# A hybrid decoder step on one core: wide state steps, later selection rounds, another order at the opening of a head pair, another last norm

## The chip, the cores and the metric

The kernel runs on one core of one Trainium2 chip, in one launch. The metric is the device time of that core in microseconds (us). The engines named below are PE (TensorE: matmuls; each has a weight load before it), DVE (VectorE), ACT (ScalarE), POOL (GpSimd) and SP (SyncE, which here only issues DMAs).

## What is computed

One decoder layer for 256 prompt tokens and 8 requests of 4 new tokens each, 288 columns in all. Everything is float32.

```python
c_rw, c_att, c_gate = split(rmsnorm(x, norm1) @ w_in)
o_rw, wkv_new, shift_new = rwkv7_mix(c_rw, ...)      # 16 heads of 64: a recurrence over tokens
#   S = S*w_t + (S a_t) b_t^T + v_t k_t^T ;  y_t = S r_t
o_att = attend(rope(q), rope(k), v, ...)             # each query keeps its 64 best keys by an indexer's scores
merged = sigmoid(g_rw) * (o_rw @ p_rw) + sigmoid(g_att) * (o_att @ p_att)
h = x + merged @ w_o
h = h + (silu(conv(gate)) * up) @ w_down             # gate, up = split(rmsnorm(h, norm2) @ w_up)
y = rmsnorm(h, norm_f)                               # also out: keys, values, states, last rows
```

## The kernel before

**Blocks.** Every weight matrix is cut into units of 128 output columns, and a unit into 16 blocks of 128 x 128 (11 for `w_down`). Weights and activations are split into a high and a low part, and a block (`blocks`, L621 to L623) is three matmuls of 128 x 128 weights on 288 columns. Per unit n, SP loads the weights into one of two slots as soon as unit n-2's low part has been made, ACT copies out the high part (`split_hi`, L587), DVE subtracts to get the low part (`split_lo`, L567, or in four parts, L579), and PE waits for that (`w_split`) before the unit's first block.

**Blocks as filling.** The attention and the recurrence have small matmuls between which DVE and ACT must work. There PE does blocks of other units meanwhile, in numbers written by hand: `fill_cols(count)` with the `FILL_...` constants in the attention (24 units, 384 blocks), `fill(count)` in a head pair (4 units, 64 blocks). A higher number at one place means a lower one later, since what is left is done at the end. DVE keeps a count of the same blocks: `streamed(count)` adds to it and issues the `split_lo` of filling unit m+2 once the count is at least 16(m+1)+5. So the place of each split in DVE's order follows from these constants. All waits are in order on each engine.

**Selection.** `eight_best` marks eight best scores (a maximum and a replacement). The second query tile's scores, `ACC[:, 1]`, take eight such rounds and two more operations (`marks_to_bias`), in `select`, which stands ahead of the six attention steps (`ATT_STEPS`: sample 0, first tile twice, second tile twice, sample 1). Their `BIASP[:, 1]` is first read in step 3.

**A head pair.** 8 passes of a loop (7 and a last one), two heads each, 64 tokens per chunk. PE opens with eight transposes of b, k, v and the read vectors into tokens-by-channels form (banks 2 and 3), then the decayed products in small tiles, `fill(5)`, and the first of the products that invert a triangular matrix (`blockwise`, L945), for which DVE must have made a mask and its transpose (`block16`). At that point DVE is still finishing the pair before: in its order stand the low part of a unit, a reciprocal and four operations on `YS`, and only then the mask. Later in the pair three state steps carry the state from chunk to chunk: PE waits for `state`, does four matmuls of 64 x 64 x 64 for the next state and four for the outputs, then `fill(2)`.

**The end.** The last norm: the square sums go through an all-ones matmul of 288 columns to all partitions (`last_sum`), DVE adds epsilon, ACT takes the root, DVE the reciprocal of 128 x 288, and multiplies `YO` by it in five parts, each of which ACT then sends out.

Of the kernel before, what the change touches and what calls it, by code (L numbers as in the profile page):

```python
# [23 lines left out]
P = 128  # L24
# [172 lines left out]
Y_PARTS = (slice(0, 4), slice(4, 8), slice(8, 12), slice(12, 14), slice(14, 16))  # L197
# [66 lines left out]
def build(nc, a, o):  # L264
# [58 lines left out]
    QZ = m("q_grouped", [P, KVH, 4, AH, DS])  # L323
    sel_at = m.at
    ACC = m("scores", [P, 2, SEQ])
# [48 lines left out]
    MT = m("chunk_map", [P, 4, CH])  # L374
# [17 lines left out]
    LO = m("l_off", [P, 2, 2 * BL])  # L392
    MLS = region(vv_at)("m_low_s", [NS, 2, NS])
# [23 lines left out]
    HRSTD = m("h_rstd", [P, N])  # L417

# [5 lines left out]
    FRSTD = m("f_rstd", [P, N])  # L424
# [22 lines left out]
    with ExitStack() as ctx:  # L447
# [34 lines left out]
        def _(sp):  # L482
            sp.dma_start(NORMS[:], a["norms"]).then_inc(sem("norms_in"), 16)

# [10 lines left out]
            load_x(12, 16, "x_in3")  # L495
# [99 lines left out]
        def _(pe):  # L595
# [281 lines left out]
            def pair(it, last=False):  # L877
# [25 lines left out]
                for w, src in enumerate((BT, KTL, RKV[:, 2, :], AR[:, 0, :])):  # L903
                    for tt in range(2):
                        ins = tr(BK[2 + tt][:, w * P:(w + 1) * P], src[:, tt * P:(tt + 1) * P], ident)  # L905
                ins.then_inc(sem("tok_mm"), 1)
# [16 lines left out]
                ins.then_inc(sem("b_mm"), 1)  # L923
                pe.wait_ge(sem("bonus"), v)
# [12 lines left out]
                fill(5)  # L937
# [11 lines left out]
                pe.wait_ge(sem("tok_sb"), v)  # L949
                pe.wait_ge(sem("block16"), v)  # L950
                settle(pe)
                blockwise(2, L1, U)
                fill(3)
                pe.wait_ge(sem("inv_l"), v * 8 - 7)
                settle(pe)
                blockwise(3, L2, UT, True)
# [3 lines left out]
                blockwise(2, L1, UT, True)  # L960
                fill(3)
                pe.wait_ge(sem("inv_l"), v * 8 - 5)
                settle(pe)
                blockwise(3, L2, T)
# [11 lines left out]
                for tt in range(2):  # L976
                    for e in range(2):
                        for par, r in enumerate(halves):
                            c0 = (0, 2 * P)[e] + tt * CH
                            mm(BK[(4, 2)[e]][halves[par ^ e], c0:c0 + CH], MK[r, 2 * e + tt, 0:CH],  # L980
                               TOK[r, tt, 2, e * HD:(e + 1) * HD], start=True, stop=True)
# [11 lines left out]
                fill(3)  # L993
                for merge in range(2):
# [44 lines left out]
                    fill(3)  # L1039
# [18 lines left out]
                fill(2)  # L1058
# [27 lines left out]
                ins.then_inc(sem("state_s_mm"), 1)  # L1086
                for c in range(1, NCH):
                    tt, par = divmod(c, 2)
# [3 lines left out]
                    settle(pe)  # L1092
                    for e, h in enumerate(halves):
                        ins = grown(grow, 0, tt, MT[h, c, :], ST[h, c - 1, :], e, par)
                    ins.then_inc(sem("state_mm"), 1)
                    if c == 1:
                        pe.wait_ge(sem("read"), v)
                        settle(pe)
                    for e, h in enumerate(halves):
                        ins = grown(read, 0, tt, ST[h, c - 1, :], QT[h, c, :], e, par)  # L1100
                ins.then_inc(sem("y_mm"), 1)
                fill(2)
                if not last:
# [110 lines left out]
            last_sum(2, FSUM, FSQ)  # L1214
# [3 lines left out]
        def _(act):  # L1218
            act.dma_start(WRAW[:, 0, 0:4, :].rearrange("p k c -> p (k c)"),
# [3 lines left out]
            for dst, src in ((PRM_ALL, "pair_params"), (LMU, "lora_mu")):  # L1223
                act.dma_start(dst[:], a[src]).then_inc(sem("params_in"), 16)

# [40 lines left out]
            act.dma_start(AC[:], a["att_c"]).then_inc(sem("att_c_lora_in"), 16)  # L1266
            actv(ROOT[:, 0:1], MEANS[:, 0:1], ACT.Sqrt)
# [203 lines left out]
            def pair(it, last=False):  # L1471
# [15 lines left out]
                act.wait_ge(sem("tok_mm"), v)  # L1487
                actv(flat(TOK[:, 0]), BK[2][:], ACT.Copy)
                actv(flat(TOK[:, 1]), BK[3][:], ACT.Copy).then_inc(sem("tok_sb"), 1)
# [9 lines left out]
                def evac(k):  # L1499
                    act.wait_ge(sem("inv_mm"), v * 8 - 8 + k)  # L1500
                    actv(flat(L2[:]), BK[2][:, 0:4 * BL], ACT.Copy).then_inc(sem("inv_u"), 1)
                act.wait_ge(sem("m1_mm"), v)
                for rows, other in both_halves:
                    ins = actv(TOK[rows, :, 1, HD:P], BK[2][other, 2 * P:3 * P].rearrange("p (t f) -> p t f", t=2), ACT.Copy)
# [161 lines left out]
            norm_root(2, FRSTD)  # L1666
# [56 lines left out]
        def _(dve):  # L1723
# [207 lines left out]
            st.done(marks_to_bias(early, BIASP[:, 0, 0:P], causal[0]))  # L1931
            select(ACC[:, 1, :], TOPK_P, BIASP[:, 1, :], causal[1], FILL_TOPK).then_inc(sem("bias_ready"), 1)
            dve.wait_ge(sem("bias_ready"), 1)

# [565 lines left out]
```

## Time and profile before

| | us |
|---|---|
| median of 3 runs | 1784.6 (1784.6 to 1786.84) |
| the profiled execution's own time | 1784.55 |
| its span | 1783.0 |
| PE busy | 1762.4 |
| DVE busy | 1119.2 |
| ACT busy | 759.8 |

A line of the time line gives start, duration, engine, line of the kernel, operation, output<-inputs, shape and count. A matmul's duration is its modelled time through the array; the next one starts before it ends, so the pace of PE is read from the starts, not from the durations or from the busy share. A float32 matmul outside the blocks is recorded as two passes, so its count is twice that of the order of instructions; a transpose is one pass.

### The profile page before, as it was taken

The page shows a single profiled execution, that of the slowest core. Times are in us where ns is not written, and L with a number is a line of the kernel's source. Part 1 is how long each engine was busy: PE and PEld are TensorE (multiplying, and loading weights), DVE is VectorE, ACT ScalarE, POOL GpSimd, SP SyncE. Part 2 cuts the span into 40 slices and gives each one's busy share as a digit, 9 for nine tenths or more (in the row PEclk, how much of TensorE's full clock was granted, in tenths as well). Part 3 has the DMA queues.
Part 4 walks back from the last instruction along what each step waited for, and adds up shares of the span by engine and source line. Part 5 has one row for each costly group of instructions (what it writes and reads, how often), then busy time and mean ns, then how long its engine had stood idle before and what let it go on. Part 6 is the DMA issues. An engine that isn't in the chain of part 4 may idle for free.

```text
span 1783.0 us, 40707 instructions
## 1 busy us (share of the span) xinstructions
PE 1762.4 (99%) x16500; PEld 1704.9 (96%) x16500; DVE 1119.2 (63%) x1995; ACT 759.8 (43%) x1059; POOL 53.6 (3%) x103
## 2 busy tenths in 40 slices
PE   9999999999999999999999999999999999999997
PEld 8999899988888888999999999999999999999996
DVE  7764954667777777765566666666666665444444
ACT  6456444555555554433443333333333333333332
POOL 2500000000000000000000000000000000000000
PEclk9999999999999999999999999999999999999999
DMA  7644344433332333644454444444444444555553
GB/s 279 227 162 163 130 160 152 155 114 107 108 107 104 111 108 113 222 166 151 174 219 165 165 165 165 165 165 165 165 165 165 165 165 162 175 169 174 169 170 132
DMA packets 51696, 283.46 MB, mean 159 GB/s; under 512 B 7248, under 2 KB 11856, under 8 KB 25776
## 3 DMA queue, kind: packets, MB, share of 16 engines
q1 hardware_dynamic: 43632, 260.35, 41.7%
q10 hardware_dynamic: 3744, 12.56, 2.0%
q0 software_dynamic: 4256, 9.65, 1.8%
q8 instruction: 46, 0.75, 0.2%
q14 instruction: 18, 0.15, 0.0%
HBM read 274.26 MB, written 8.27 MB: 158 GB/s over the span
## 4 chain that ended last, share of the span: by engine, by line
PE 95%; DVE 3%; DMA 1%; ACT 0%; issue 0%; DVEq 0%; SPq 0%
PE bank L621 30%; PE bank L623 28%; PE bank L622 28%; PE bank L945 1%; PE bank L985 1%; DVE w_lo L567 1%; DVE scores L1919 1%; PE bank L852 0%; PE bank L905 0%; DVE max L1886 0%; DMA x_raw<-in_x 0%; PE bank L800 0%; PE bank L817 0%; PE bank L1046 0%; PE bank L642 0%
## 5 line engine op out<-in xcount | busy, mean ns | idle before, releaser
L621 PE MATMUL bank<-x_split,w_lo 128*128 128x288 f32 x2880 | 873.2, 303 | 3.3 <-DVE w_lo L567 2.1
L622 PE MATMUL bank<-x_split,w_hi 128*128 128x288 f32 x2880 | 849.5, 295 | 0.0
L623 PE MATMUL bank<-x_split,w_hi 128*128 128x288 f32 x2880 | 847.0, 294 | 0.0
L587 ACT ACTIVATE w_hi<-w_raw 128x2048 fp32r<-128x2048 f32 (+1 forms) x262 | 468.8, 1789 | 590.9 <-PE bank L623 578.7
L567 DVE TENSOR_TENSOR w_lo<-w_raw,w_hi 128x2048 fp32r<-128x2048 f32 (+1 forms) x238 | 503.8, 2117 | 283.7 <-ACT w_hi L587 283.4
L621 PEld LDWEIGHTS bank<-x_split,w_lo 128*128 128x128 f32 x2880 | 540.2, 188 | 20.3 <-issue 9.6
L622 PEld LDWEIGHTS bank<-x_split,w_hi 128*128 128x128 f32 x2880 | 541.0, 188 | 1.8 <-issue 0.7
L623 PEld LDWEIGHTS bank<-x_split,w_hi 128*128 128x128 f32 x2880 | 542.2, 188 | 0.0
L621 PE MATMUL bank<-act_split,w_lo 128*128 128x288 f32 x704 | 208.5, 296 | 0.0
L622 PE MATMUL bank<-act_split,w_hi 128*128 128x288 f32 x704 | 207.7, 295 | 0.0
L623 PE MATMUL bank<-act_split,w_hi 128*128 128x288 f32 x704 | 207.0, 294 | 0.0
L623 PEld LDWEIGHTS bank<-act_split,w_hi 128*128 128x128 f32 x704 | 132.6, 188 | 0.0
L622 PEld LDWEIGHTS bank<-act_split,w_hi 128*128 128x128 f32 x704 | 132.2, 188 | 0.0
L621 PEld LDWEIGHTS bank<-act_split,w_lo 128*128 128x128 f32 x704 | 131.9, 187 | 0.2 <-DVE w_lo L567 0.2
L621 PE MATMUL bank<-merged_split,w_lo 128*128 128x288 f32 x256 | 75.9, 297 | 0.0
L622 PE MATMUL bank<-merged_split,w_hi 128*128 128x288 f32 x256 | 75.5, 295 | 0.0
L623 PE MATMUL bank<-merged_split,w_hi 128*128 128x288 f32 x256 | 75.3, 294 | 0.0
L579 DVE TENSOR_TENSOR w_lo<-w_raw,w_hi 128x512 fp32r<-128x512 f32 x96 | 62.1, 682 | 1.2
L2356 DVE TENSOR_TENSOR conv<-bank,h_rstd 128x288 f32<-128x288 f32 x44 | 20.1, 457 | 67.8 <-PE bank L623 67.8
L1301 ACT ACTIVATE cols<-bank 128x256 f32<-128x256 f32 x40 | 15.4, 384 | 90.6 <-PE bank L623 90.6
L2339 DVE TENSOR_TENSOR gate_ext<-bank,h_rstd 128x256 f32<-128x256 f32 x44 | 18.7, 425 | 52.9 <-PE bank L623 52.9
L621 PEld LDWEIGHTS bank<-merged_split,w_lo 128*128 128x128 f32 x256 | 48.0, 187 | 0.4 <-issue 0.2
(390 smaller groups left out, 1537.9 us busy)
## 6 DMA issues: line engine op xcount, KB each, us to landing
w_raw<-in_w_up SPq DMA_DIRECT2D x88, 1024.0 KB, 4.8
w_raw<-in_w_in SPq DMA_DIRECT2D x47, 1024.0 KB, 4.9
w_raw<-in_w_down SPq DMA_DIRECT2D x64, 704.0 KB, 4.0
w_raw<-in_w_gate SPq DMA_DIRECT2D x32, 1024.0 KB, 4.9
w_raw<-in_w_p SPq DMA_DIRECT2D x16, 1024.0 KB, 4.8
w_raw<-in_w_o SPq DMA_DIRECT2D x16, 1024.0 KB, 4.8
h<-in_x ACTq DMA_DIRECT2D x1, 2304.0 KB, 10.3
h_spill<-h ACTq DMA_DIRECT2D x1, 2304.0 KB, 9.6
```

The costliest lines, as they stand in the source:

```text
L567: eng.tensor_tensor(WLO[:, slot, 0:kt], WRAW[:, slot, 0:kt], WHI[:, slot, 0:kt].bitcast(F32), ALU.subtract).then_inc(sem("w_split"), 1)
L579: ins = dve.tensor_tensor(WLO[:, slot, k], WRAW[:, slot, k], WHI[:, slot, k].bitcast(F32), ALU.subtract)
L587: actv(WHI[:, slot, 0:kt], WRAW[:, slot, 0:kt], ACT.Copy).then_inc(sem("w_hi"), 3 if isinstance(n, int) and n == 2 else 1)
L621: mm(out, wl, hi, start=first and k == ks[0], stop=False, skip_group_check=True)
L622: mm(out, w, lo, start=False, stop=False, skip_group_check=True)
L623: ins = mm(out, w, hi, start=False, stop=last and k == ks[-1], skip_group_check=True)
L945: ins = mm(BK[bank][q, u * w:(u + 1) * w], lhs[q, u], rhs[q, u], start=True, stop=True)
L985: return mm(BK[banks[par]][halves[e], c0:c0 + CH], lhs, rhs, start=start, stop=False, skip_group_check=True)
L1301: actv(tile[:, 1:1 + SEQ], BK[j % 2][:, 0:SEQ], ACT.Copy)
L1919: ins = V.scalar_tensor_tensor(acc, src, w, acc if i or par else causal[qt], ALU.mult, ALU.add)
L2339: V.tensor_tensor(gx[:, 2:2 + SEQ], BK[0][:, 0:SEQ], HRSTD[:, 0:SEQ], ALU.mult)
L2356: st.done(V.tensor_tensor(c[:, 0:N], BK[1][:, 0:N], HRSTD[:], ALU.mult))
```

## The change

The parts, in program order:

- Start: the norm gains are loaded by ACT's queue, no longer first by SP's; two parameter loads of ACT move later; SP issues the last quarter of `x` behind the load of unit 2, and the constants behind the load of unit 3.
- Attention: the constants of the filling change (selection of the samples 25 to 33 blocks, `FILL_TOPK` 30 to 12, `FILL_SAMPLE` 14 to 16, `FILL_SOFTMAX` 14 to 15). The eight rounds of the second tile are taken out of `select` and put into the attention steps: three after the probabilities of step 0, two after the maximum of step 1, three and the bias after the probabilities of step 1.
- Pair: the products stand first; of the transposes k and v follow them and b and a come later, behind the third inversion product; `fill(5)` goes, and the five blocks are given to `fill` calls further on and to the rest at the end (15 to 16 blocks).
- State steps: the map and the state are kept as 128 x 128 matrices with zeros off the two heads' blocks, and a step is one matmul of 128 x 128 weights on 64 columns. The outputs of a chunk come one step later.
- Last norm: the sums are taken to tokens-by-two form, root and reciprocal are of 128 x 6, and three diagonal matrices and three matmuls spread the result; `YO` is multiplied from the bank, in parts of 2, 3, 4, 4 and 3 tiles.

```diff
-Y_PARTS = (slice(0, 4), slice(4, 8), slice(8, 12), slice(12, 14), slice(14, 16))
+Y_PARTS = (slice(0, 2), slice(2, 5), slice(5, 9), slice(9, 13), slice(13, 16))
-FILL_ROPE, FILL_REQUESTS, FILL_TOPK_S, FILL_TOPK, FILL_SAMPLE = 12, 2, 25, 30, 14
+FILL_ROPE, FILL_REQUESTS, FILL_TOPK_S, FILL_TOPK, FILL_SAMPLE = 12, 2, 33, 12, 16
-FILL_SCORES, FILL_SOFTMAX, FILL_P_T, FILL_PV = 8, 14, 5, 4
+FILL_SCORES, FILL_SOFTMAX, FILL_P_T, FILL_PV = 8, 15, 5, 4
...
                 if isinstance(n, int) and n == 2:
+                    load_x(12, 16, "x_in3")
+                if isinstance(n, int) and n == 3:
                     sp.dma_start(MC[:], a["main_c"]).then_inc(sem("main_c_in"), 16)
...
                 for c in range(1, NCH):
                     fill(2)
+                    if c > 1:
+                        pe.wait_ge(sem("read"), v * 4 - 4 + c)
+                        both_heads(read, c - 1, STB[:, c % 2, :], QT[:, c - 1, :])
                     pe.wait_ge(sem("state"), v * 4 - 4 + c)
                     pe.wait_ge(sem("map"), v)
+                    both_heads(grow, c, MTB[:, c - 1, :], ST[:, c - 1, :]).then_inc(sem("state_mm"), 1)
...
+                    if which == 0:
+                        late_rounds(0, 3)
                     streamed(FILL_SCORES + FILL_SOFTMAX)
...
+                if n == 1:
+                    late_rounds(5, 8)
+                    st.done(marks_to_bias(late, BIASP[:, 1, :], causal[1]))
                 streamed(FILL_SCORES + FILL_SOFTMAX)
...
+            for tt in range(3):
+                V.tensor_scalar(FDIAG[:, tt, :], ident, FROOT[:, tt, 0:1], float(D_MODEL), ALU.mult, ALU.mult).then_inc(sem("norm_ms"), 1)
```

On PE at the opening of a pair in the loop, before (`b_t`, `k_t`, `rkv`, `ar` on the constants are the transposes, `ar,b_t` and the like the products, `u_and_t,l` the inversion):

```order
L1137 UNCONDITIONAL_BRANCH
L1137 ISA
L905 MATMUL bank<-main_consts,b_t 128x128 x2
L905 MATMUL bank<-main_consts,k_t 128x128 x2
L905 MATMUL bank<-main_consts,rkv 128x128 x2
L905 MATMUL bank<-main_consts,ar 128x128 x2
L912 MATMUL bank<-ar,b_t 32x32 x16
L916 MATMUL bank<-ar,b_t 64x64 x8
L921 MATMUL bank<-ar,k_t 64x128 x8
L929 MATMUL bank<-b_t,ar 64x32 x8
L933 MATMUL bank<-ar_s,bk_v_s 64x64 x2
L936 MATMUL bank<-main_consts,bk_v_s 128x128
```

Five blocks and then L945 follow. The same place now:

```order
L1145 UNCONDITIONAL_BRANCH
L1145 ISA
L919 MATMUL bank<-ar,b_t 32x32 x16
L923 MATMUL bank<-ar,b_t 64x64 x8
L928 MATMUL bank<-ar,k_t 64x128 x8
L912 MATMUL bank<-main_consts,k_t 128x128 x2
L912 MATMUL bank<-main_consts,rkv 128x128 x2
L937 MATMUL bank<-b_t,ar 64x32 x8
L941 MATMUL bank<-ar_s,bk_v_s 64x64 x2
L944 MATMUL bank<-main_consts,bk_v_s 128x128
L952 MATMUL bank<-u_and_t,l_108 32x32 x16
```

The first inversion product stands right behind the opening, and four of the eight transposes are gone from it.

On DVE in attention steps 0 and 1, before (the splits are `w_lo`):

```order
L1948 SCALAR_TENSOR_TENSOR prob<-softmax_stats,att_consts 128x16
L1951 TENSOR_SCALAR prob<-prob,softmax_stats 128x256
L567 TENSOR_TENSOR w_lo<-w_raw,w_hi 128x2048
L1958 SCALAR_TENSOR_TENSOR prob<-bank,bias_prompt 128x512
L1962 TENSOR_REDUCE softmax_stats<-prob 128x4
L567 TENSOR_TENSOR w_lo<-w_raw,w_hi 128x2048
L1965 RECIPROCAL softmax_stats<-softmax_stats 128x4
```

And now:

```order
L1980 TENSOR_SCALAR prob<-prob,softmax_stats 128x256
L1910 MAX max_79<-scores 128x8
L1913 MATCH_REPLACE scores<-max_79,scores 128x256
L1910 MAX max_79<-scores 128x8
L1913 MATCH_REPLACE scores<-max_79,scores 128x256
L1910 MAX max_79<-scores 128x8
L1913 MATCH_REPLACE scores<-max_79,scores 128x256
L571 TENSOR_TENSOR w_lo<-w_raw,w_hi 128x2048 x2
L1989 SCALAR_TENSOR_TENSOR prob<-bank,bias_prompt 128x512
L1993 TENSOR_REDUCE softmax_stats<-prob 128x4
```

Three rounds stand between the probabilities of step 0 and the splits, and two splits stand together.

## Rows read from the trace of the kernel before

**Rows 1.** The page: span, then busy time of each engine.
```profile
span 1783.0 us, 40707 instructions
PE 1762.4 (99%) x16500; PEld 1704.9 (96%) x16500; DVE 1119.2 (63%) x1995; ACT 759.8 (43%) x1059; POOL 53.6 (3%) x103
```
**Rows 2.** Time line of PE (start, us, operation, count), from one pair into the next.
```profile
482.18 0.65 PE L1111 MATMUL bank<-y,main_consts 128*128 128x288 f32 x2
...
494.77 0.38 PE L905 MATMUL bank<-main_consts,b_t 128*128 128x128 f32 x2
...
495.73 0.35 PE L912 MATMUL bank<-ar,b_t 64*32 64x32 f32 x32
...
497.27 0.38 PE L621 MATMUL bank<-x_split,w_lo 128*128 128x288 f32 x1
...
499.57 0.45 PE L945 MATMUL bank<-u_and_t,l 32*32 32x32 f32 x32
```
**Rows 3.** Time line of DVE in the same stretch.
```profile
482.94 0.46 DVE L2221 SCALAR_TENSOR_TENSOR y<-bank,y 128x288 f32<-128x288 f32 x1 [1.14 <-PE bank L1111]
...
487.23 1.95 DVE L2054 RECIPROCAL squares_k<-squares_k 128x288 f32<-128x288 f32 x1
...
494.58 1.95 DVE L2235 RECIPROCAL y_sq<-y_sq 128x288 f32<-128x288 f32 x1
...
499.15 0.31 DVE L2106 STREAM_TRANSPOSE l<-u_and_t 128x128 f32<-128x128 f32 x1
```
**Rows 4.** Time line of PE: a state step, and the end of the three.
```profile
521.24 0.33 PE L985 MATMUL bank<-state,chunk_map 64*64 64x64 f32 x4
521.62 0.40 PE L621 MATMUL bank<-x_split,w_lo 128*128 128x288 f32 x1
...
522.61 0.33 PE L985 MATMUL bank<-state,chunk_map 64*64 64x64 f32 x4
...
525.45 0.82 PE L852 MATMUL bank<-lora,cols 128*128 128x128 f32 x5
```
**Rows 5.** Time line of PE: six float32 passes with 128 x 128 weights, then a block.
```profile
485.23 0.61 PE L870 MATMUL bank<-main_consts,decay_tok 128*128 128x130 f32 x4
485.67 0.31 PE L871 MATMUL bank<-main_consts,decay_tok 128*128 128x40 f32 x2
485.81 0.38 PE L621 MATMUL bank<-x_split,w_lo 128*128 128x288 f32 x1
486.03 0.29 PE L622 MATMUL bank<-x_split,w_hi 128*128 128x288 f32 x1
```
**Rows 6.** Time line of DVE: two rounds' starts, and the probabilities of step 0.
```profile
221.82 0.43 DVE L1886 MAX8 max<-scores 128x8 f32<-128x256 f32 x1
...
222.80 0.43 DVE L1886 MAX8 max<-scores 128x8 f32<-128x256 f32 x1
...
239.88 0.35 DVE L1951 TENSOR_SCALAR prob<-prob,softmax_stats 128x256 f32<-128x256 f32 x1
```
**Rows 7.** Time line of ACT: the unit's end at 234.79, and the first exponential.
```profile
234.79 0.39 ACT L1301 ACTIVATE cols<-bank 128x256 f32<-128x256 f32 x1 [2.02 <-PE bank L623]
...
238.86 0.48 ACT L1377 ACTIVATE prob<-bank,softmax_stats 128x260 f32<-128x260 f32 x1
```
**Rows 8.** Time line of PE in the selection: its longest wait for a split.
```profile
218.90 0.40 PE L621 MATMUL bank<-x_split,w_lo 128*128 128x288 f32 x1 [0.89 <-DVE w_lo L567]
```
**Rows 9.** Time line of PE in the first 34 us: the wait for unit 2.
```profile
23.04 0.40 PE L642 MATMUL bank<-x_split,w_lo 128*128 128x288 f32 x1 [1.36 <-DVE w_lo L567]
```
**Rows 10.** Time line of PE and DVE in the last norm.
```profile
1770.17 0.75 PE L610 MATMUL bank<-f_squares,mean_ones 128*128 128x288 f32 x2 [0.53 <-ACT f_squares L1658]
...
1771.93 1.95 DVE L1737 RECIPROCAL f_rstd<-f_rstd 128x288 f32<-128x288 f32 x1 [0.51 <-ACT f_rstd L1274]
1773.91 5.23 DVE L2394 TENSOR_TENSOR y_out<-y_out,f_rstd 128x1152 f32<-128x1152 f32 x5
```
**Rows 11.** Stretches after the last matmul: us, PE busy (x), granted clock, DMA share, GB/s.
```profile
1771.00:1775.40 4.40, 0.00 (x0) 1.00 0.00 0
1775.40:1783.00 7.60, 0.00 (x0) 0.50 0.77 310
```

More of the change, by code:

```diff
@@ L902, in pair, with turned @@
                 pe.wait_ge(sem("ar_ready"), v)
[L903 to L906, printed above, removed]
+                settle(pe)
+                def turned(bank, sources):
+                    for w, src in enumerate(sources):
+                        for tt in range(2):
+                            ins = tr(BK[bank][:, (2 * tt + w) * P:(2 * tt + w + 1) * P], src[:, tt * P:(tt + 1) * P], ident)
+                    ins.then_inc(sem("tok_mm"), 1)
                 chunks = [(tt, par) for tt in range(2) for par in range(2)]
@@ L1086, in pair, with both_heads @@
                 ins.then_inc(sem("state_s_mm"), 1)
+                def both_heads(banks, c, lhs, rhs):
+                    tt, par = divmod(c, 2)
+                    return mm(BK[banks[par]][:, tt * CH:(tt + 1) * CH], lhs, rhs, start=False, stop=False, skip_group_check=True)
                 for c in range(1, NCH):
-                    tt, par = divmod(c, 2)
                     fill(2)
+                    if c > 1:
+                        pe.wait_ge(sem("read"), v * 4 - 4 + c)
+                        both_heads(read, c - 1, STB[:, c % 2, :], QT[:, c - 1, :])
                     pe.wait_ge(sem("state"), v * 4 - 4 + c)
                     pe.wait_ge(sem("map"), v)
[L1092 to L1101, printed above, removed]
+                    both_heads(grow, c, MTB[:, c - 1, :], ST[:, c - 1, :]).then_inc(sem("state_mm"), 1)
                 fill(2)
+                pe.wait_ge(sem("read"), v * 4)
+                both_heads(read, NCH - 1, STB[:, 0, :], QT[:, NCH - 1, :]).then_inc(sem("y_mm"), 1)
                 if not last:
@@ L1501, in evac @@
                     actv(flat(L2[:]), BK[2][:, 0:4 * BL], ACT.Copy).then_inc(sem("inv_u"), 1)
+                act.wait_ge(sem("tok_mm"), v * 2)
+                actv(TOK[:, :, 0:4:3, :], BK[6][:].rearrange("p (t w f) -> p t w f", t=2, w=2), ACT.Copy).then_inc(sem("tok_sb"), 1)
                 act.wait_ge(sem("m1_mm"), v)
                 for rows, other in both_halves:
[L1504 removed]
+                    ins = actv(TOK[rows, :, 1, HD:P], BK[3][other, 2 * P:3 * P].rearrange("p (t f) -> p t f", t=2), ACT.Copy)
                 ins.then_inc(sem("m1_odd"), 1)
@@ L1665, in _ @@
             down_units(KT // 2 - 1, 2 * DU - 2)
-            norm_root(2, FRSTD)
+            act.wait_ge(sem("norm_sq_used"), KT * 3)
+            actv(FROOT[:].rearrange("p t x -> p (t x)"), BK[2][:, 0:6], ACT.Sqrt, bias=EPSC[:]).then_inc(sem("norm_rms"), 1)
             for i, k in enumerate(Y_PARTS):
@@ L1930, in _, with late_rounds @@
                     eight_best(early, TOPK_P - 8 * heads[1])
-            st.done(marks_to_bias(early, BIASP[:, 0, 0:P], causal[0]))
-            select(ACC[:, 1, :], TOPK_P, BIASP[:, 1, :], causal[1], FILL_TOPK).then_inc(sem("bias_ready"), 1)
+            marks_to_bias(early, BIASP[:, 0, 0:P], causal[0]).then_inc(sem("bias_ready"), 1)
             dve.wait_ge(sem("bias_ready"), 1)
+            streamed(FILL_TOPK)
+            late = ACC[:, 1, :]
+            def late_rounds(r0, r1):
+                for r in range(r0, r1):
+                    eight_best(late, TOPK_P - 8 * r)
             for n, (kind, which) in enumerate(ATT_STEPS):
@@ L2147, in pair @@
                 inv(4)
-                add_t(blocks(3), 4)
+                add_t(blocks(2), 4)
                 V.transpose(L1[:], T).then_inc(sem("inv_l"), 1)
@@ L2183, in pair, with state_blocks @@
                 split_part(dve, n + 2, 0, 3)
+                def state_blocks(c):
+                    tt, par = divmod(c, 2)
+                    for e, h in enumerate(halves):
+                        ins = V.tensor_scalar(STB[h, c % 2, e * HD:(e + 1) * HD], BK[6 + par][h, tt * CH:(tt + 1) * CH],
+                                              PC[h, c:c + 1], None, ALU.mult)
+                    ins.then_inc(sem("read"), 1)
                 def state(c):
```

97 lines of the change are left out of this document (65 added, 32 removed).

## The prediction

> **What bounds the kernel now.** I read the page first [rows 1]: PE is busy for 1762.4 of a span of 1783.0 us, no other engine for two thirds of it. That share is modelled, so the second look is at PE's starts. A block is three matmuls, and in long runs of blocks their starts stand 0.133 apart, so a block costs 0.40 us. Every microsecond that PE spends on something new, or waits, is added to the time; work of DVE or ACT counts only where PE waits for it. The third look is for those places: the opening [rows 9], the selection [rows 8], the end [rows 10], and one that is nearly a wait: DVE's stretch from one pair into the next [rows 3]. Everything is reckoned against the profiled execution's own 1784.55 us (span 1783.0 plus 1.55 around it), within 0.1 of the median of 1784.6. A measurement of this kernel can tell about 0.2%, 3.6 us, from no change.
>
> **Pair openings, seven times.** On DVE the tail of the old pair and the mask of the new one form a fixed stretch. It starts when PE's L1111 has run (DVE's L2221 at 482.94), is unbroken from 487.23, and delivers the transposed mask at 499.15 + 0.31 = 499.46 [rows 3]: 16.5 us, which the change leaves in the same order. PE's L945 starts at 499.57, just behind it [rows 2, 3]. On PE before, the last block ends at 494.77, the opening takes 2.50 (to 497.27), five blocks 2.00, and 0.30 is left for a switch of tile size and a wait of about 0.2 [rows 2]. So DVE is already last here, and the five blocks are what covers it. After: one more block of the rest ahead (+0.40); the opening without four of its eight transposes (their eight plus one switch take 0.96, so −0.43), with one more change from tiles to whole matrices and back (+0.19, below) and a last switch (0.09) takes 2.35. PE is ready at 494.77 + 0.40 + 2.35 = 497.52 and waits for 2.05, until 499.57. The blocks are not lost: four more stand further on in the pair, where they cost 1.60, and the four transposes cost 0.43 there. The pair grows by 2.05 of wait less the 0.15 to 0.2 waited before: **+1.9 x 7 = +13.3** (the first pair has no tail ahead). The bounds: the wait is 1.6 if DVE's stretch starts a little earlier relative to PE, 2.3 if the moved evacuations of the transposes cost something elsewhere: +11 to +15.
>
> **Switches of tile size.** Between two state steps PE does two blocks: 0.99 from 521.62 to 522.61 instead of 0.80 [rows 4]. I take the 0.19 as the price of going from whole matrices to tiles and back. The transposes behind the third inversion product and the second group in the opening add one such pair to each of 8 pairs: **+1.5**.
>
> **State steps, eight times.** A step costs 8 small passes, 0.38 (521.24 to 521.62) plus 0.19 for the switches; the three with their six blocks take 521.24 to 525.45 = 4.21, of which 2.40 are blocks, and with the switch in front the steps cost 1.89 [rows 4]. About 0.1 of that is a wait at the end. After: six matmuls of 128 x 128 weights, two passes each. Such a pass is not in the old steps; the nearest row is six passes on 130 and 40 columns, 485.23 to the first block, whose second matmul starts at 486.03: 486.03 − 0.133 − 485.23 = 0.67, or 0.111 each [rows 5]. So 12 x 0.111 = 1.33, without switches, and 0.1 of wait: 1.43, a gain of 0.45 a pair, **−3.6**. The lower end: passes on 64 columns at the pace of the small steps' 0.38 / 8 = 0.048 give 0.6, a gain of 1.2 a pair (−9). The upper end: DVE makes six more small operations, and the waits for `state` grow to 0.5 a pair: +0.5. The value is taken near the row with wide weights, since the weights and not the columns set such short passes. The Trainium skill ("TensorEngine Tiling (Array Packing)", section "Key Properties") says that different tiles can load weights and multiply in parallel. The rows agree, with 0.048 for a small pass and 0.111 for a wide one. By that rule alone a product would be four tiled passes, 0.19, against two wide ones, 0.22, and the gain would be the switches only.
>
> **Attention.** The eight late rounds leave the selection, where PE waited three times, the longest 0.89 by the row [rows 8], 2.4 in all by the starts: −2.4. But they go in front of splits. A round is 0.98 (221.82 to 222.80), three are 2.94 [rows 6]. The selection now ends after 128 instead of 136 blocks. ACT is in order, and at a unit's end it waits for PE's last block of it: the `cols` at 234.79 [rows 7] is 8 blocks after the selection before and lies at its end now. From there ACT needs to 238.86 for the exponential, and DVE has the probabilities at 239.88 + 0.35 = 240.23: 5.4 behind the unit's end, called T [rows 6, 7]. Now three rounds and a split of 2.2 to 2.3 (492.39 to 494.58 is another one of the same kind) follow: ready at T + 5.4 + 2.94 + 2.3 + small gaps = T + 10.9. PE needs it for block 144: 8 blocks, the scores (0.9) and 8 more, T + 7.4. Wait 3.6. In step 1 the chain repeats with a probability set later, three rounds and a bias of 0.75 ahead of the next split: ready 20.1 after the first split is, PE there after 16.0. Wait 4.1. Third: with these constants the count behind step 3 is 244, one short of the 245 that releases the split of the next filling unit, so it moves behind the probabilities of step 4; PE waits some 1.7. Sum 9.4 − 2.4 = **+7.0**. The bounds are +2 (each wait 1.6 shorter, if ACT's exponential comes earlier than I place it) and +9.
>
> **Opening.** PE's wait of 1.36 at 23.04 is for the low part of unit 2 [rows 9], whose load stands behind the last quarter of `x` (576 KB). The DMAs move about 0.41 MB per us there, so the load comes 1.4 earlier, and ACT stands idle there: **−1.5** by PE's starts, between −0.3 (if another split is late next) and −1.9.
>
> **Last norm.** Before: L610 at 1770.17, 0.5 to the reciprocal's start at 1771.93, 1.95, then the first part of `YO` at 1773.91, whose transfer starts at 1775.31 [rows 10]; in the last stretch the DMAs move 310 GB/s and are 77% busy [rows 11]. After: root and reciprocal of 6 columns (0.2 each, as the small operations in [rows 6] and their neighbours), three diagonals, six short matmuls, and a first part of 2 tiles instead of 4: ready about 1773.3. From there the 2.36 MB of output set the end: **−1.8** (−0.8 to −2.3).
>
> **Sum.** −1.5 + 7.0 + 13.3 + 1.5 − 3.6 − 1.8 = +14.9: 1784.55 + 14.9 = 1799.4, say **1799**.
>
> **The rivals.**
> *No wait at the openings.* The blocks taken out would only pay if DVE's stretch were shorter than it looks, because some of it waits for PE's products and these come earlier now. For it: the mask does read a product. Against it: from 487.23 DVE does not stop. Then 14.9 − 13.3 = +1.6, 1786.2. Chance 10%, counted as "within".
> *The rounds are hidden.* If the first probabilities stand ready well before T + 5.4, the split waits shrink to little or nothing: 7.0 falls to 0 or −2.4, and the time is 1790 to 1792.5. For it: the scores of step 0 come earlier relative to T. Against it: `cols`, exponential and probabilities are in a row on ACT and DVE, with a table load of 1.3 in front. Chance 15%.
> *The clock falls.* A wait of 3.6 or 4.1 of PE could bring the granted clock from 2.4 to 1.2 GHz. What the trace shows: after the last matmul it stayed at 1.00 for the whole stretch from 1771.00 to 1775.40 and stood at 0.50 in the next [rows 11]. So waits of 4 stay just inside. If it fell, the blocks after each wait would run at half pace for a while: for 4 us of them, +2 for each of two waits, 1803. Chance 10%. The Trainium skill speaks for this rival ("TensorE: Matmul & The Clock Gate", section "HAM oscillation — how this bites in real kernels"): waits between matmuls can bring the clock down to half, again and again.
> *DVE keeps up at both places: faster.* If the mask is ready by 497.5, that is if DVE's stretch shrinks by 2.0 from its 16.5, seven waits vanish and also the old ones of 0.15 (−1.0), and the freed DVE takes the rounds for nothing: −1.5 − 2.4 − 3.6 + 1.5 − 1.0 − 1.8 = −8.8, 1776. It decides at 2.0 us of slack in DVE's stretch, of which the rows show none. Chance 5%.
>
> **How the numbers follow.** The main case has 60%: its terms' bounds, not all at one end, give 1794 to 1805. The rounds hidden 15%, the clock 10% (inside the same range), no wait 10%, faster 5%. Range for 8 in 10: from 1789, which takes in the hidden rounds, to 1805. Left out are no wait and faster, 15%, and a little above. Faster by over 0.2% (under 1781.0): 6%. Within: 7% of the 10%, since a part of the no-wait case lies above 1788.1. Slower: 87%.
>
> **What would show each step.** In the profile of after: PE's first inversion product waits about 2.0 for DVE's mask in seven of eight pairs, and a pair takes some 1.7 more. In the attention PE waits three times for a `w_lo`, 3.6, 4.1 and 1.7; in the selection it no longer does. The wait at 23 is gone. Two blocks and a state step take 0.80 + 0.44. The first part of `y` is sent about 2 earlier. The clock is 1.00 up to the last matmul. I am wrong above all if the wait at the openings is not there, since it is nearly all of the sum, or if its seven instances differ, which would mean that I took one pair's DVE order for all.

## The result, and the profile after

| | before | changed |
|---|---|---|
| median | 1784.6 | 1815.4 (1812.4 to 1816.4) |
| ratio | | 1.0168, 95% interval 1.0151 to 1.0186 |
| span of the profiled execution | 1783.0 | 1812.8 |
| PE busy | 1762.4 | 1770.8 |

The kernel became slower, as forecast, but by 31 us and not by 15, outside the range of 1789 to 1805. The page of the changed kernel, the lines that answer to [rows 1], and its clock:

```profile
span 1812.8 us, 40614 instructions
PE 1770.8 (98%) x16418; PEld 1719.0 (95%) x16418; DVE 1136.5 (63%) x2064; ACT 760.3 (42%) x1059; POOL 53.8 (3%) x103
...
PEclk9999989999999999999999999999999999999999
```

The sixth slice, 227 to 272 us, is under 9 tenths; that is the attention. A slice of 45 us hides the shorter dips. The four largest of PE's waits are these (engine, line, releaser: us in total, times, longest):

```profile
PE bank L952 <- DVE l L2142: 12.9, 7, 1.9
PE bank L625 <- DVE w_lo L571: 10.2, 4, 3.8
PE bank L856 <- DVE state_s L2259: 4.2, 7, 0.6
PE bank L646 <- DVE x_split L1773: 1.8, 1, 1.8
```

**Where the 29.8 us of span came from.** I compare the time between matmuls that both kernels have, by their starts in us.

| stretch | before | changed | difference | forecast |
|---|---|---|---|---|
| to the first rotation of the 128 x 128 `cols` (71.78 in both) | 71.78 | 71.78 | 0.0 | −1.5 |
| from there to the first pair's opening | 288.03 | 301.39 | +13.4 | +7.0 |
| the eight pairs, to the last mean of `y` | 346.64 | 364.46 | +17.8 | +11.2 |
| from there to the end | 1076.55 | 1075.17 | −1.4 | −1.8 |

**The pairs.** PE's time line at two pair openings, and DVE's ahead of the first, as [rows 2, 3]:

```profile
422.62 0.55 PE L952 MATMUL bank<-u_and_t,l 32*32 32x32 f32 x32 [1.91 <-DVE l L2142]
471.01 0.45 PE L952 MATMUL bank<-u_and_t,l 32*32 32x32 f32 x32 [1.84 <-DVE l L2142]
```
```profile
417.54 1.95 DVE L2285 RECIPROCAL y_sq<-y_sq 128x288 f32<-128x288 f32 x1
...
422.16 0.31 DVE L2142 STREAM_TRANSPOSE l<-u_and_t 128x128 f32<-128x128 f32 x1
```

The wait is there seven times, 1.74 to 1.91, and stands where it was forecast: DVE still finishes the old pair. But the pairs are of two kinds. From L952 to the next L952 they take 48.4, 46.95, 48.4, 48.3, 46.95 and 48.3 us, against 45.0 before. The windows behind the two waits above tell why (stretch, us, busy time and count of PE, weight load, DVE, ACT, POOL, granted clock, DMA share, GB/s):

```profile
422.62:425.62 3.00, 3.00 (x45) 2.66 (x49) 2.03 (x10) 1.34 (x5) 0.00 (x0) 0.54 0.00 0
471.01:474.01 3.00, 3.00 (x78) 2.70 (x79) 2.55 (x13) 1.42 (x5) 0.00 (x0) 1.00 0.00 0
```

Behind the first, PE ran at half clock, 1.2 GHz, for nearly all of the stretch (the mean granted clock is 0.54), and issued 45 matmuls where it issued 78 behind the second. PE is "busy" for all 3.00 us in both, so the busy share shows nothing of it. In the pace it is plain: the single matmuls of a block start 0.24 apart instead of 0.133. Four of the seven waits are followed by such a stretch of some 3 us, which costs 1.4.

**The attention.** Its four new waits, and the windows behind three of them:

```profile
242.56 0.61 PE L625 MATMUL bank<-x_split,w_lo 128*128 128x288 f32 x1 [3.39 <-DVE w_lo L571]
265.38 0.40 PE L625 MATMUL bank<-x_split,w_lo 128*128 128x288 f32 x1 [3.76 <-DVE w_lo L571]
309.21 0.40 PE L625 MATMUL bank<-x_split,w_lo 128*128 128x288 f32 x1 [1.45 <-DVE w_lo L571]
343.51 0.40 PE L625 MATMUL bank<-x_split,w_lo 128*128 128x288 f32 x1 [1.56 <-DVE w_lo L571]
```
```profile
242.56:247.56 5.00, 5.00 (x21) 5.00 (x21) 2.15 (x1) 0.00 (x0) 0.00 (x0) 0.50 0.75 279
309.21:312.21 3.00, 3.00 (x22) 3.00 (x23) 2.10 (x1) 0.86 (x1) 0.00 (x0) 1.00 0.69 197
343.51:346.51 3.00, 3.00 (x22) 3.00 (x23) 2.71 (x5) 0.76 (x1) 0.59 (x1) 1.00 0.63 188
```

Three were forecast (3.6, 4.1, 1.7). The fourth was not. The clock stays at half for 6.2 us behind the first long wait and for 3.4 behind the second; there the matmuls of the blocks stand 0.24 apart, and about 4.4 us are lost. By the starts the four waits are 10.6; with 4.4 of half clock, 0.4 at L866 and the 2.4 that went from the selection that makes +13.0 of the 13.4. ACT's line of the unit's end (T in the forecast), and DVE's time line, which shows what the rounds stood in front of, and what they could have filled instead:

```profile
231.91 0.39 ACT L1323 ACTIVATE cols<-bank 128x256 f32<-128x256 f32 x1 [5.84 <-PE bank L627]
```
```profile
226.47 2.28 DVE L571 TENSOR_TENSOR w_lo<-w_raw,w_hi 128x2048 fp32r<-128x2048 f32 x1
236.59 0.17 DVE L1975 COPY softmax_stats<-prob 128x4 f32<-128x4 f32 x1 [7.83 <-ACT prob L1399]
...
237.01 0.35 DVE L1980 TENSOR_SCALAR prob<-prob,softmax_stats 128x256 f32<-128x256 f32 x1
237.27 0.42 DVE L1910 MAX8 max<-scores 128x8 f32<-128x256 f32 x1
...
240.22 4.49 DVE L571 TENSOR_TENSOR w_lo<-w_raw,w_hi 128x2048 fp32r<-128x2048 f32 x2
```

DVE was idle for 7.83 us waiting for the exponential, then did three rounds, and only then the split for which PE waited.

**The start and the end.** The wait of [rows 9] is gone. PE's first block waits 1.8 instead of 0.7 and starts at 8.48 instead of 7.45:

```profile
8.48 0.37 PE L646 MATMUL bank<-x_split,w_lo 128*128 128x288 f32 x1 [1.81 <-DVE x_split L1773]
```

Behind it the granted clock was 0.50 from 9.82 to 13.23, a third place with a stretch at half clock.

In the last norm the parts of `y` are multiplied from 1803.92 and sent from 1804.71; reckoned from PE's last matmul of `w_down`, the end is 1.4 nearer than in [rows 10]:

```profile
1802.69 0.68 DVE L2447 TENSOR_SCALAR f_diag<-main_consts,f_root 128x128 f32<-128x128 f32 x3
1803.92 5.21 DVE L2451 TENSOR_TENSOR y_out<-y_out,bank 128x576 f32<-128x576 f32 x5 [0.56 <-PE bank L1234]
```

### The profile page after: what moved, and what is told of

The parts are those of the page before. It is cut to its first block, busy times and chain, and to the rows that moved or that the text cites. A ratio compares the mean times of both kernels' runs of the same rounds, so it can differ in the third digit from the quotient of the medians.

```text
span 1812.8 us, 40614 instructions
## 1 busy us (share of the span) xinstructions
PE 1770.8 (98%) x16418; PEld 1719.0 (95%) x16418; DVE 1136.5 (63%) x2064; ACT 760.3 (42%) x1059; POOL 53.8 (3%) x103
## 4 chain that ended last, share of the span: by engine, by line
PE 89%; DVE 7%; ACT 2%; issue 1%; DMA 0%; DVEq 0%; ACTq 0%
PE bank L625 28%; PE bank L627 26%; PE bank L626 26%; DVE w_lo L571 1%; PE bank L952 1%; DVE squares_k L2090 1%; DVE y_sq L2285 1%; PE bank L994 1%; ACT L1556 0%; PE bank L646 0%; PE bank L647 0%; PE bank L648 0%; DMA w_raw<-in_w_in 0%; ACT w_hi L591 0%; PE bank L856 0%
## 5 line engine op out<-in xcount | busy, mean ns | idle before, releaser
L591 ACT ACTIVATE w_hi<-w_raw 128x2048 fp32r<-128x2048 f32 (+1 forms) x262 | 468.8, 1789 | 589.4 <-PE bank L627 575.6
L627 PEld LDWEIGHTS bank<-merged_split,w_hi 128*128 128x128 f32 x256 | 48.2, 188 | 0.0
## 6 DMA issues: line engine op xcount, KB each, us to landing
h<-in_x ACTq DMA_DIRECT2D x1, 2304.0 KB, 11.2
```

The source lines that it names most:

```text
L591: actv(WHI[:, slot, 0:kt], WRAW[:, slot, 0:kt], ACT.Copy).then_inc(sem("w_hi"), 3 if isinstance(n, int) and n == 2 else 1)
L627: ins = mm(out, w, hi, start=False, stop=last and k == ks[-1], skip_group_check=True)
```

## The experiments

Medians are given with the ratio to the kernel before, run on the same chip, and its 95% interval. "Half clock in k of 7" counts the pair waits with a stretch at half clock behind them in the profiled execution.

**Only the attention undone: `no_att`.**

> The changed kernel with the selection and the attention as before (all eight rounds in the selection, the old filling constants); everything else as changed. Theory, waits and clock: the attention's stretch from 200 us to the first pair opening is 14.6 longer in the changed kernel, 8.3 to 10 of it waits of PE for a low part and the rest blocks at half the clock behind the two long ones; all of it goes: 1815.4 - 14.6 = 1800.8, granted clock 1.00 up to the first pair's end. Rival, the stretch is longer since more blocks and switches lie in it: the moved blocks come back elsewhere and the time falls by less than 10, to 1806 or more.

1801.85, ratio 1.0103 (1.0087 to 1.0120): 13.5 less than with it. The selection's old waits are back (0.64, 0.90, 0.57), no wait stands between them and the first pair, and the pairs are as in the changed kernel: waits of 1.74 to 1.89, half clock in 4 of 7. So the change of the attention costs 13.5 on its own. The loss came from waits and clock, and not from the number of blocks.

**The five blocks back at the opening: `open5`.** And two, or one, of them: `open2`, `open1`. The first line of the edit is that of `open5`; in `open2` and `open1` it is `fill(2)` and `fill(1)`. The second is one of the places further on from which blocks were taken back.

```diff
+                fill(5)
                 pe.wait_ge(sem("block16"), v)
...
-                fill(4)
+                fill(3)
```

> The changed kernel with the five blocks back ahead of the first inversion product (four of them taken from the places further on in the pair, one from the rest). Theory, waits and clock: the wait of 1.85 in seven pairs shrinks to 0.2 and a pair to 46.95 - 1.65 = 45.3 us; the clock, which stood at half for 3 us behind four of the seven waits (1.4 us each), stays at 1.00: 7 x 1.65 + 4 x 1.4 = 17, so 1798.4. Rival, the clock falls because the small products now stand packed at the start of the opening: the half-clock stretches stay, 1804.

> The changed kernel with two of the five blocks back ahead of the first inversion product (both taken from places further on in the pair). The wait in seven pairs goes from 1.85 to 1.05 and an undisturbed pair from 46.95 to 46.15, -5.6. Theory: a wait of 1.05 doesn't bring the clock down (behind the attention's waits of 1.45 and 1.56 it stood at 1.00), so the four stretches at half clock go too, -5.6: 1804.2. Rival: any wait at this place does, if it lies so: 1 to 4 stretches stay, 1806 to 1810.

> The changed kernel with one of the five blocks back ahead of the first inversion product (taken from behind the third product). The wait in seven pairs is 1.45: between 1.05, behind which the clock stood at 1.00 in all seven, and 1.85, behind which it fell in three or four of seven. An undisturbed pair takes 46.55, -2.8 in all. Theory: how often the clock falls depends on how long the wait is, and at 1.45 it falls in 0 to 2 of 7 pairs: 1807 to 1809.5. Rival: the small tiles around the wait matter and not its length alone; 3 or more pairs at half clock, 1811 or more.

| blocks ahead | wait | half clock | median, us | ratio (95%) |
|---|---|---|---|---|
| 0 (changed kernel) | 1.85 | 4 of 7 | 1815.4 | 1.0168 (1.0151 to 1.0186) |
| 1 | 1.45 | 3 of 7 | 1810.95 | 1.0149 (1.0134 to 1.0165) |
| 2 | 1.05 | 0 of 7 | 1801.9 | 1.0092 (1.0075 to 1.0109) |
| 5 | 0.25 | 0 of 7 | 1798.65 | 1.0080 (1.0063 to 1.0097) |

The waits go down by 0.40 for each block, as a DVE stretch of fixed length demands (the fifth comes from the rest, which stands ahead of the wait too). The second block saved 9.05 us: 2.8 in waits, 4.2 in three stretches at half clock, and 1.2 of the rest in a shorter one in the attention. With one block back, two openings of the same execution:

```profile
470.60:473.60 3.00, 3.00 (x41) 2.69 (x41) 2.03 (x10) 1.41 (x5) 0.00 (x0) 0.51 0.00 0
518.57:521.57 3.00, 3.00 (x78) 2.70 (x79) 2.54 (x13) 1.40 (x5) 0.00 (x0) 1.00 0.00 0
```

The waits ahead of these two are 1.45 and 1.47. The length of the wait does not decide alone, then: the two waits are alike, and so is what stands around them. I had expected 0 to 2 stretches at 1.45, and it was 3; the rival (3 or more, 1811) gave the number. The attention's waits of 1.45 and 1.56 brought no half clock in any of the six executions that have them. These stand between whole-array blocks, the pair's wait between small products. That fits the rival that the surroundings count, but no run changed the surroundings alone. The surroundings can't be all of it either: of the first long wait of the attention, 3.4 in each of seven executions with the same blocks around it, six had half clock behind them and the one in `busywait` had not. At which moment a wait falls may count too; no run moved a wait alone, so what picks out the waits stays open.

**Work without use in the wait: `busywait`, `busywait8`.** PE does matmuls whose result nobody reads, in the time in which it waited.

```diff
+                for _ in range(8):
+                    mm(BK[3][:, 0:P], ident, mean_ones, start=True, stop=True)
                 pe.wait_ge(sem("block16"), v)
```

> The changed kernel with 13 matmuls of 128 x 128 x 128 without use ahead of the first inversion product, so that PE works through the time in which it waited (about 1.8 us). Theory, the idle engine is what brings the clock down: DVE is as late as before, no time is won from the waits, but the half-clock stretches behind them go: -4 x 1.4, and +1.8 in the first pair, which had no wait: 1811.5; periods of the pairs all near 46.95. Rival, the clock goes by something else (the mix of tile sizes, other engines): two kinds of pairs stay, 48.3 and 46.95, and the time is 1817.

> The changed kernel with 8 matmuls of 128 x 128 x 128 without use ahead of the first inversion product. In the run with 13 of them two passes cost 0.23 us each, 3.0 in all: the clock was 1.00 in all pairs, but PE was then 1.0 late in each. 8 take 1.84 and just fill the wait of 1.85. Theory, the idle engine brings the clock down: all pairs take 46.95 to 47.1, no stretch at half clock behind the openings: 1815.4 - 4 x 1.4 + 1.8 in the first pair, which had no wait, = 1811.6. Rival, the overshoot of 1.0 and not the work was what kept the clock up: pairs of 48.3 come back, 1817.

With 13: 1818.07, ratio 1.0193 (1.0176 to 1.0210), not the 1811.5 that I had expected. I had sized them at 1.8 us; they took 3.0, so this run was PE-bound at the opening, with the clock at 1.00 in all pairs and every pair 47.93 long. The time is near the rival's 1817, but its two kinds of pairs are not there. With 8: 1810.17, 1.0140 (1.0123 to 1.0157), 5.2 less than the changed kernel, although eight times 2 us of useless work were added, one of them (the first pair's) where there was no wait to fill. PE's time line and the window behind:

```profile
421.55 1.95 PE L957 MATMUL bank<-mean_ones,main_consts 128*128 128x128 f32 x16
423.59 0.45 PE L952 MATMUL bank<-u_and_t,l 32*32 32x32 f32 x32
```
```profile
423.59:426.59 3.00, 3.00 (x78) 2.71 (x79) 2.55 (x13) 1.38 (x5) 0.00 (x0) 1.00 0.00 0
```

All pairs take 46.83 to 46.98. The first inversion product starts when DVE lets it, as before; only the clock is different. This shows the half clock behind the openings to come of PE standing idle, and not of DVE, the tiles or the order of the products. Not all of the 5.2 us is owed to that. In the profiled executions the pairs take 3.9 less (360.55 against 364.46, from the first opening to the last mean of `y`). Another 1.2 come from a shorter half-clock stretch in the attention, where the edit changed nothing: that part is luck.

**The pair's part alone on the kernel before: `pair_only`.**

> The kernel before with only the new opening of a pair and its moved blocks; selection, attention, state steps, start and last norm as before. Theory: this part alone brings the seven waits of 1.85, a pair grows by 1.85, and behind some of the waits (2 to 6 of 7) the clock stands at half for 3 us, 1.4 each: 1784.2 + 13.3 + 5.6 = 1803, 1800 to 1806. Rival: the waits of DVE come from the whole change (the wide state steps have put DVE's stretch later), and without them they are under 1.5 and the time is under 1799.

1801.9, ratio 1.0101 (1.0085 to 1.0116): waits of 1.73 to 1.88, half clock in 4 of 7. So the wait is not owed to the state steps.

**The two thresholds: `lag`.**

```diff
-                streamed(FILL_P_T + (FILL_PV if n == 1 else 0))
+                streamed(FILL_P_T + (FILL_PV if n == 1 else 0), 4)
...
-            streamed(FILL_P_T + FILL_PV, EARLY_LAG)
+            streamed(FILL_P_T + FILL_PV, 0)
```

> The changed kernel, in which DVE issues a split one block earlier in the attention steps ahead of the exponential (244 blocks are then enough, 245 are not needed) and two blocks earlier behind the last step (304 instead of 306). Theory: the waits of 1.45 (block 256) and 1.56 (block 320) of the changed kernel are there only because the new constants fall short of these two thresholds by one and by two; both splits go back ahead of the operations they stood behind, both waits go and the one of 0.4 behind them (L866): 1815.4 - 3.4 = 1812.0. Rival: the late rounds have put DVE behind, and the waits shrink by half at most: 1814.

1811.62, ratio 1.0142 (1.0125 to 1.0159). Both waits are gone from the trace, the 0.39 at L866 has stayed, and half clock came in 5 of 7 pairs instead of 4. In the changed kernel counts that are one and two short had put a split of 2.29 us behind DVE's next waits, for an exponential in one place and for ACT's `cols` in the other.

**The rounds where DVE is idle: `ahead`, `ahead2`.** The edit is that of `ahead2`, in step 0. Both runs also move the last three rounds and the bias of step 1 ahead of its exponential and lower the thresholds, the last one as in `lag`.

```diff
                     streamed(FILL_P_T if n else FILL_SAMPLE)
+                    if which == 0:
+                        late_rounds(0, 5)
+                        streamed(0, 0)
                     dve.wait_ge(sem("exp"), n + 1)
...
-                    if which == 0:
-                        late_rounds(0, 3)
```

> The changed kernel with the late rounds moved ahead of DVE's waits for the exponential (five in step 0, where DVE is idle for 7.8 us, three and the bias in step 1, where it is idle for 6.3), the split of the finished unit right behind them, and the last threshold two blocks lower. Theory: nothing is then in front of the splits; the waits of 3.4, 3.8, 1.45 and 1.56, the two stretches at half clock behind the long ones (4.4) and 0.4 at L866 go, 15 in all: 1800 to 1801, and PE doesn't wait in the selection either. Rival: ACT, which takes a unit's end only when PE is done with it, holds the splits, and the rounds' place decides little: 1808 or more.

> As the run with the rounds ahead of the exponentials, with one difference: the split that is due in step 0 stands ahead of the five rounds, and only the next one behind them. In that run the first split had gone behind the rounds, and PE waited 1.86 at block 128, with half clock behind it. Theory: this last wait of the attention goes: 1815.4 - 10.9 (four waits by the starts) - 4.4 (half clock) = 1800.1, granted clock 1.00 up to the first pair's end. Rival: the rounds and the split don't fit into DVE's idle time there, and the exponential's probabilities come late: 1802 or more.

`ahead`: 1803.37, ratio 1.0094 (1.0078 to 1.0111). One wait was left, 1.86 at block 128, and behind it the clock fell. Here I had put five rounds ahead of a split that was already due (the one of 226.47 above), the mistake of the changed kernel on a smaller scale. `ahead2`, with that split first: 1799.97, ratio 1.0084 (1.0069 to 1.0099), as expected (1800.1). No wait of PE for a split is left from the selection to the first pair, and from 71.8 us to the first opening it takes 2.1 us less than the kernel before, in spite of 0.4 at L866. The late rounds were a good idea; their place was wrong.

**The state steps: `b_steps`, `steps_mix`.** The first is the kernel before with the wide state steps alone. The edit shown is what the second has beyond it: two mixing operations of DVE stand behind the grown states instead of ahead of them.

```diff
-                    if c == 2 and not last:
-                        mix_prev(it + 1, 0)
...
+                    mix_prev(it + 1, 0)
                     st.mark(mix_prev(it + 1, 2))
```

> The kernel before with only the wide state steps. Theory from the trace of the changed kernel: the steps themselves are 0.5 shorter a pair, but DVE, with six more small operations in a row, is late with the grown sample states by 0.6, against 0.1: +0.1 a pair, 1784.6 + 0.8 = 1785.4, within 0.2% of before. Rival, as forecast: the wait is not bound to the steps, and they gain 0.45 a pair: 1781.

> The kernel before with the wide state steps, and one mixing operation pair of DVE (0.7 us) put behind the grown sample states instead of ahead of the last state. Theory: the wait of 0.58 behind the state steps was DVE's excess of work there; it shrinks to 0.1 or less, and the matmuls' gain of 0.5 a pair comes through: 1784.1 - 7 x 0.5 = 1780.6. Rival: the next thing that waits for DVE there (the centred outputs) takes the gain back: 1784.

`b_steps`: 1784.07, ratio 1.0002 (0.9992 to 1.0012); a pair takes 45.12 instead of 45.01. `steps_mix`: 1781.11, ratio 0.9985 (0.9976 to 0.9994); a pair takes 44.65. PE's wait of 0.6 for the grown states is there in `b_steps` and is 0.1 in `steps_mix`. DVE's line of the grown states and PE's next line in the changed kernel, and then in `steps_mix`:

```profile
450.94 0.74 DVE L2259 TENSOR_TENSOR state_s<-state_s,bank 128x256 f32<-128x256 f32 x2
...
451.83 0.93 PE L856 MATMUL bank<-lora,cols 128*128 128x128 f32 x6 [0.60 <-DVE state_s L2259]
```
```profile
434.91 0.74 DVE L2223 TENSOR_TENSOR state_s<-state_s,bank 128x256 f32<-128x256 f32 x2
...
435.79 0.93 PE L855 MATMUL bank<-lora,cols 128*128 128x128 f32 x6
```

**The start: `start_only`, `start_sp`.** The second leaves the norm gains first in SP's queue.

> The kernel before with only the new start: norm gains by ACT's queue, two parameter loads of ACT later, the last quarter of x behind unit 2, the constants behind unit 3. The trace of the changed kernel shows both of its effects: the wait of 1.36 at 23 us is gone, but ACT's first part of the weights lands 1.6 later, PE waits 1.8 to 2.0 ahead of its first block instead of 0.7, and the clock is 0.79 from 8 to 16 us; at 71.78 us both kernels are at the same matmul. Theory: the start gains nothing, 1783.8 (within 0.5). Rival, as forecast: -1.5, 1782.3, and something else in the changed kernel took it back.

> As the last, but the norm gains stay first in SP's queue; x, unit 2 and the constants in the new order, the two parameter loads later. Theory: it is the norm gains ahead of the first weights in ACT's queue that hold the first block; without that the first w_hi starts near 5.0 again and only the gain is left: -1.4, 1782.4, and the matmul at 71.8 comes 1 to 1.5 earlier. Rival: the first block is held by x, not by the weights, and nothing changes: 1783.8.

`start_only`: 1785.4, ratio 1.0004 (0.9995 to 1.0013). `start_sp`: 1783.96, ratio 0.9997 (0.9988 to 1.0006), with its eleven runs spread from 1781.2 to 1786.9. The traces differ more than the medians. ACT's first part of the weights, `start_only` and then `start_sp`:

```profile
6.82 0.63 ACT L1238 ACTIVATE w_hi<-w_raw 128x512 fp32r<-128x512 f32 x1 [2.30 <-DMA w_raw<-in_w_in]
```
```profile
4.96 0.63 ACT L1239 ACTIVATE w_hi<-w_raw 128x512 fp32r<-128x512 f32 x1 [0.54 <-DMA w_raw<-in_w_in]
```

A load of 24 KB ahead of the first weights in ACT's queue holds them back by 1.9. The matmul at 71.78 comes at 71.59 in `start_only` and at 69.42 in `start_sp`. In all traces PE's first block starts at 7.3 to 7.8 with the gains in SP's queue and at 8.4 to 8.9 with them first in ACT's. In `best2`, below, which has the order of `start_sp`, the matmul at 71.78 comes at 69.63. So two traces show the gain of 2 us; the medians of `start_sp` and of the kernel before can't tell it from none.

**Together: `best`, `best2`.** New last norm, wide state steps with the mixing behind, rounds as in `ahead2`, a pair's opening as before; `best2` has the norm gains in SP's queue.

> The kernel before with the new start and last norm, the wide state steps with the mixing operation behind, and the late rounds as in the last run but one (ahead of the exponentials, the due split first), the opening of a pair as before. Theory: 1784.2 - 1.25 (start) - 1.35 (last norm) - 3.5 (state steps) - 2.4 (no waits in the selection, none in the attention) = 1775.7. Rival: a part takes the place of another (the selection, without its waits, meets a load that is late; a half-clock stretch comes in): 1778 or more.

> The combined kernel (new last norm, wide state steps with the mixing operation behind, late rounds ahead of the exponentials, opening of a pair as before) with the norm gains first in SP's queue again. Theory: the start then gives 1.4, which it did not in the combined kernel before: 1778.4 - 1.4 = 1777.0. Rival: no change, 1778.4.

`best`: 1778.4, ratio 0.9967 (0.9955 to 0.9980). `best2`: 1777.28, ratio 0.9959 (0.9945 to 0.9972). Both beat both kernels. `best` missed its expectation by 2.7: 1.25 of that was the start, which I had still counted as a gain then, 0.8 the steps, which gave 2.7 and not 3.5; the rest is within the scatter.

## Why the prediction was wrong, point by point

**Right.** What bounds the kernel; the two places where waits would arise, and their size. Pair opening: forecast 2.05, measured 1.85 (the wait of before was 0.1 and not 0.15 to 0.2). Attention, forecast 3.6, 4.1 and 1.7, measured 3.4, 3.8 and 1.45. The chain behind the first holds step by step: the unit's end on ACT at 231.91, probabilities at 237.36 (T + 5.4, as forecast), split ready at 242.5 (T + 10.6 against 10.9). An undisturbed pair grew by 1.95, forecast 1.7. That is partly luck: the opening with its switch of tile size was forecast at 2.1 and gave 1.83 in `pair_only`, and the state steps, forecast at −0.45, gave +0.1.

**The step that failed most: "waits of 4 stay just inside".** I took the end of the trace of before, where the clock stood at 1.00 through 4.4 us of idle time [rows 11], as a bound on all waits, thought of the fall only for the two long ones, and gave it 10%. It came behind both of these and behind four of the seven waits of 1.85: 4.4 + 5.6 = 10 us in the changed kernel, where the sum had nothing and the rival 4. These 10 us are two thirds of the miss of 14.9; the rest is 2.0 in the attention, 1.5 at the start, 1.0 in the pairs and 0.4 in the last norm. One instance of an idle stretch is no bound: of seven equal waits three left the clock alone. `busywait8` shows the cause and its price: with the waits filled the pairs take 3.9 less, in spite of 2 more in the first. What "TensorE: Matmul & The Clock Gate" of the Trainium skill says in its section "HAM oscillation — how this bites in real kernels", that waits between matmuls can bring the clock to half again and again, is what these traces show, and it should have had the larger chance. The waits of its example are of 3 to 5 us; that waits of 1.45 and 1.85 can do it is shown by these runs and not by the page.

**State steps.** The term of −0.45 a pair was right for PE (−0.36 in `steps_mix`) and wrong in the changed kernel (+0.1 in `b_steps`). The failed step is "0.1 of wait": I had DVE's six operations fit into idle time. There was too little: DVE now works from 445.50 almost without a stop until the grown states at 451.7, and PE waits 0.60. The upper end that I gave (waits of 0.5 a pair) was the truth. Products of two wide passes started 0.14 to 0.20 apart, those of four tiled ones 0.17 to 0.21 [rows 4]: the two kinds of product cost nearly the same, and what the wide form won is mostly the switches, as the forecast's last sentence on the steps had it. The 0.111 of [rows 5] was a mean of unlike passes: four with 130 columns start 0.111 apart, the two with 40 take 0.07 each.

**Attention.** Besides the clock, a threshold: I worked out that the count stood one short at one place, and did not go on to the last one, where it is two short (304 against 306). It cost 1.56 of wait, and the 0.4 at L866 was not in the sum either. `lag`, where both short waits are gone, shows that the counts made them.

**Start.** The term −1.5 was wrong. I looked at what the change moves back in SP's queue, not at what it puts ahead in ACT's: norm gains in front of the first weights, whose high part starts 1.6 later in the changed kernel. The half clock behind PE's first block is not owed to this alone: `steps_mix`, with the old start, has it too, behind a wait of 1.83. Gain and loss cancel, as `start_only` shows.

**Last norm.** Forecast −1.8, measured −1.4: the sending starts 1.7 nearer to the last block, but the transfers end only 1.4 earlier.

**Rivals.** No wait at the openings, the hidden rounds and a faster kernel all fell: each was told apart by the four lines of waits above. The clock rival was the right one, and at 4 us it had less than half of the size.

## What to carry to other kernels

A wait of the bounding matmul engine costs its own length and can cost clock on top, here 1.4 us behind 26 of the 42 pair waits of 1.7 to 1.9: sum both before work that covers a wait is moved away. Take away cover only where the trace shows the other engine ahead; here [rows 3] showed DVE without a gap, and two blocks of cover out of five were already enough to keep the clock. New work on a second engine belongs into its idle time ahead of a wait, behind what is already due; and where counts release work, recount every threshold when a constant changes.

## What the runs showed of the hardware

The clock fell to half around or behind idle times of PE of 1.45 (3 of 7) and 1.85 (4 or 5 of 7 in six executions) at the pair openings. It never did so at those of 1.05 or less, and not at 1.45 to 1.56 between whole blocks (12 waits in six executions). Of the waits of 3.4 in the attention one, in `busywait`, left it at 1.00. It stayed low for some 3 us behind a pair's wait, and for 6.2 behind the first long wait of the attention in the changed kernel. Eight useless products a pair kept it up and cost less than the half clock. In the rows of `busywait8` two passes with 128 x 128 weights and 128 columns start 0.112 apart; those of the state steps, with 64 columns, 0.055 to 0.112. What sets this was not separated.
